# Sample attention of a hybrid decoder step: scores one step behind the key transposes, probabilities scaled by row on the copy out, selection started earlier, first gathers spread

## The reference, cut to what matters

```python
kc = concat([block_means(past_c), block_means(kvc)])        # 128 block means a sample
o_c, imp = compressed_branch(qg, kc, q_pos)                 # softmax over the means; imp = its probabilities, summed
idx, valid = select_blocks(imp, q_pos, n_sel)               # the 8 best of 64 blocks of 64 rows, first and current forced
o_s = sel_attend(qg, kv_sel, idx, valid, q_pos)             # softmax over the selected blocks' rows
o_w, win_new = window_sample(qg, win_buf, kvw, q_pos)       # softmax over the last 512 rows
g = sigmoid(ngate)
o = g[..., 0:1] * o_c + g[..., 1:2] * o_s + g[..., 2:3] * o_w
```

## Time and profile before

| | us |
|---|---|
| median of 3 runs | 1898.01 |
| lowest, highest | 1890.36, 1906.17 |
| the profiled execution | 1902.42 |
| its span in the trace | 1900.3 |
| its busy times: PE, PEld, DVE, ACT, POOL | 1733.5, 1214.2, 955.4, 521.6, 626.8 |
| DMA: bytes moved, mean rate | 248.81 MB, 131 GB/s |

### The profile page before, as it was taken

The page is one execution under the profiler, slowest core; times in us unless marked ns, Lnnn a source line. Parts: engine busy times, 40 slices in busy tenths (PEclk is TensorE's granted clock), DMA queues, the critical chain, the costliest instruction groups (busy, mean ns, idle before and its releaser), DMA issues.

```text
span 1900.3 us, 25684 instructions
## 1 busy us (share of the span) xinstructions
PE 1733.5 (91%) x9632; PEld 1214.2 (64%) x9632; DVE 955.4 (50%) x1708; ACT 521.6 (27%) x1109; POOL 626.8 (33%) x630
## 2 busy tenths in 40 slices
PE   7999999998999689966888889998999999999996
PEld 6777777777877455643555556775467777763332
DVE  5778767773000477744445444233367777750003
ACT  3222212220111345533444445211222223220101
POOL 2344443351000422245555552130055565630000
PEclk9999999998999899987999999999989999999998
DMA  7766666663541100025667668252052322221211
GB/s 243 244 234 228 218 233 220 222 241 109 158 109 34 45 1 1 2 78 165 207 208 222 217 214 257 92 140 75 28 133 67 85 71 74 82 67 56 67 42 50
DMA packets 201014, 248.81 MB, mean 131 GB/s; under 512 B 32201, under 2 KB 173850, under 8 KB 192538
## 3 DMA queue, kind: packets, MB, share of 16 engines
q1 hardware_dynamic: 178556, 137.70, 24.7%
q0 software_dynamic: 21248, 109.46, 16.6%
q10 hardware_dynamic: 1088, 0.00, 0.0%
HBM read 236.09 MB, written 19.29 MB: 134 GB/s over the span
## 4 chain that ended last, share of the span: by engine, by line
PE 74%; DVE 11%; issue 5%; DMA 5%; ACT 4%; another core or an unknown queue 1%; POOL 0%; SPq 0%; DVEq 0%; ACTq 0%; POOLq 0%
PE ps L2200 21%; PE ps L2325 8%; PE ps L2149 5%; DVE mem L1267 5%; DMA mem<-in_cache_cmp_kv,pidx 4%; PE ps L1781 4%; PE ps L2174 4%; PE ps L1770 3%; PE ps L2264 3%; PE ps L1970 3%; PE ps L2113 3%; PE ps L1802 2%; PE ps L2062 2%; PE ps L2029 2%; PE ps L2016 2%
## 5 line engine op out<-in xcount | busy, mean ns | idle before, releaser
L2200 PE MATMUL ps<-mem 128*128 128x288 f32 x1296 | 324.7, 408 | 0.8 <-DVE mem L1205 0.8
L2200 PEld LDWEIGHTS ps<-mem 128*128 128x128 f32 x1296 | 245.5, 191 | 67.7 <-DVE mem L1205 1.0
L759 POOL DMA_INDIRECT mem<-in_cache_sel_kv,sidx x192 | 183.7, 957 | 311.6 <-PE ps L1970 158.8
L1770 PE MATMUL ps<-mem 128*128 128x288 f32 x768 | 208.7, 434 | 16.3 <-DVE mem L1293 15.3
L1770 PEld LDWEIGHTS ps<-mem 128*128 128x128 f32 x768 | 155.7, 205 | 62.2 <-issue 16.2
L1267 DVE TENSOR_TENSOR mem<-mem 128x2048 f32<-128x2048 f32 x56 | 163.7, 2924 | 38.3 <-DMA mem<-in_cache_cmp_kv,pidx 37.6
L722 POOL DMA_INDIRECT mem<-in_cache_cmp_kv,pidx x56 | 90.5, 1616 | 238.3 <-DVE mem L1267 206.6
L2325 PE MATMUL ps<-mem 128*128 128x512 f32 x352 | 163.8, 609 | 0.0
L2174 PE MATMUL ps<-mem 128*64 128x512 f32 x288 | 82.3, 647 | 59.1 <-ACT mem L1048 32.3
L1552 DVE TENSOR_TENSOR mem<-ps,mem 128x512 f32<-128x512 f32 x64 | 44.2, 691 | 159.4 <-PE ps L2174 103.1
L2325 PEld LDWEIGHTS ps<-mem 128*128 128x128 f32 x352 | 63.9, 191 | 80.7 <-issue 80.6
(11 more groups left out here) (372 smaller groups left out, 2776.2 us busy)
## 6 DMA issues: line engine op xcount, KB each, us to landing
mem<-in_cache_sel_kv SPq DMA_DIRECT2D x320, 128.0 KB
mem<-in_w_up SPq DMA_DIRECT2D x44, 512.0 KB, 4.6
mem<-in_w_in SPq DMA_DIRECT2D x32, 512.0 KB, 10.0
mem<-in_w_in SPq DMA_DIRECT2D x14, 1024.0 KB, 9.2
mem<-in_w_down SPq DMA_DIRECT2D x10, 1024.0 KB, 5.0
mem<-in_state_win_kv SPq DMA_DIRECT2D x16, 512.0 KB
out<-in_state_win_kv POOLq DMA_DIRECT2D x8, 1008.0 KB, 15.7
mem<-in_x_prompt SPq DMA_DIRECT2D x8, 512.0 KB, 5.4
```

The lines of the kernel that those rows point to most:

```text
L759: pool.indirect_dma_start(kring[kq % NKR][:, j, :], None, pool_rows, bass.IndirectOffsetOnAxis(sidx[:, i:i + 1], 0)).then_inc(pg_g[kq % NK ...
L1770: mm = t.matmul(ps[:, 2 * (u % 2) + a, 0:NHF], lhs(k), hT[:, k, a * NHF:(a + 1) * NHF], start=(k == 0), stop=(k == KD - 1))
L2200: mm = t.matmul(ps[:, bank, 0:NHF], lhs[:, k, :], rhs[:, k, :], start=(first and k == 0), stop=(k == KD // 2 - 1), skip_group_check=True)
```

## The change

Scores of step n are now issued at the end of step n+1 (`scores`), after the next piece's transposes; keys are copied out by half, each half with its own count, into three buffers in turn (the third in `avm` and `scanm`, free by then). The probabilities are no longer multiplied by gate over sum (`e_scale` is gone): selected and window values are added up side by side in `obank`, now two banks in turn, and `e_out` multiplies by row as it copies out and adds the compressed branch, which is computed by itself (`e_cv`, `e_cmp`). P(m) has one PSUM bank in place of two. `LAG` is 14 in place of 16. The selection's first two parts are one step earlier and two others one step later on PE. The 12 early gathers stand one after each second step of the prompt's attention. POOL waits for the states' stores before it issues the window's copies, since both now share one semaphore.

```diff
-LAG = NC + 6
+LAG = NC + 4
-        kTs = [view(2 * PGC * P).rearrange("p (g n) -> p g n", g=2) for _ in range(2)]
+        kTs = [[view(PGC * P) for _ in range(2)] for _ in range(2)]
+        kTs.append([avm[:, :, :, :].rearrange("p i r c -> p (i r c)"), scanm[:, 0:PGC * P]])
-        obank = ps[:, 6, :]
+        obank = [ps[:, 5 + q, 0:2 * P] for q in range(2)]
...
@@ POOL
+            pool.wait_ge(state_out, 32 * HH)
             for b in range(SB):
                 pool.dma_start(win_s[0, b, 0:WIN - ST].rearrange("w h g d -> w (h g d)"),
...
-            for kq in range(KAHEAD):
-                e_gather(kq)
+            early = [(kq, (j,)) for kq in range(KAHEAD) for j in K_POOL]
             for m, (i, gp, r, br) in enumerate(STEPS):
...
+                if m % 2 and 16 < m < 16 + 2 * len(early) + 1:
+                    e_gather(*early[(m - 16) // 2])
@@ ACT
-                    act.wait_ge(ek_ok, kq + 1)
-                    if kq >= 2:
-                        bb, cc = divmod(kq - 2, NPC + 1)
+                    if kq >= 3:
+                        bb, cc = divmod(kq - 3, NPC + 1)
                         act.wait_ge(es_ok, NC * bb + cc + 1)
-                    a.activation(kTs[kq % 2], ps[:, 0:2, :], ACT.Copy).then_inc(ekT_ok, 1)
+                    for gp in range(2):
+                        act.wait_ge(ek_ok, 2 * kq + gp + 1)
+                        a.activation(kTs[kq % 3][gp], ps[:, gp, :], ACT.Copy).then_inc(ekT_ok, 1)
...
-                    if c == 3:
+                    if c == 2:
                         e_c2(b + 1)
...
-                if c < 4 and 0 < b <= SB:
-                    e_exp(b - 1, [c] if c < 3 else [3, 4])
+                if 1 <= c < 5 and 0 < b <= SB:
+                    e_exp(b - 1, [c - 1] if c < 4 else [3, 4])
@@ DVE
-            def e_scale(b, pieces):
-                for k in pieces:
-                    for q, (a, n) in enumerate(PIECES[k]):
-                        x = sc[b % 2][:, a:a + n]
-                        ins = v.tensor_scalar(x, x, est[:, b % 2, 20 + (q > 0):21 + (q > 0)], None, ALU.mult)
-                    ins.then_inc(epn_ok, 1)
+            def e_cmp(b):
+                dve.wait_ge(cv_ok, b + 1)
+                v.tensor_scalar(ocmp[b % 3], cbank[:, 256:384], gateq[:, b, 0:1], 1.0 / CB, ALU.mult, ALU.mult).then_inc(ocmp_ok, 1)
             def e_out(b):
                 dve.wait_ge(epv_ok, NC * (b + 1))
+                dve.wait_ge(ecf_ok, b + 1)
+                dve.wait_ge(ocmp_ok, b + 1)
+                o, w = ocmp[b % 3], obank[b % 2]
+                link(v.scalar_tensor_tensor(o, w[:, 0:P], est[:, b % 2, 20:21], o, ALU.mult, ALU.add))
                 for g in range(G):
...
+                if c == 1 and b < SB:
+                    e_cmp(b)
                 if b + 1 < SB:
-                    if c == 4:
+                    if c == 3:
                         e_c4(b + 1)
@@ PE
             def e_c1(b):
-                wait(pe, pq_ok, b)
+                wait(pe, ocmp_ok, b)
...
+            def e_cv(b):
+                pe.wait_ge(c10_ok, b + 1)
+                pe.wait_ge(pq_ok, b + 1)
+                for gp in range(2):
+                    mm = t.matmul(cbank[gp * S:(gp + 1) * S, 256:384], pscT[:, gp * S:(gp + 1) * S],
+                                  cmt[:, b, KV + gp * P:KV + (gp + 1) * P], start=True, stop=True)
+                mm.then_inc(cv_ok, 1)
...
+            def scores(n):
+                b, c = divmod(n, NC)
+                kq = b * (NPC + 1) + c
+                wait(pe, esc_ok, n - 1)
+                for gp in range(2):
+                    out = ps[64 * gp:64 * gp + 64, 2 + n % 2, :]
+                    if c <= NPC:
+                        pe.wait_ge(ekT_ok, 2 * kq + gp + 1)
+                        mm = t.matmul(out, qbd[:, b, gp, :], kTs[kq % 3][gp], start=True, stop=True)
...
-                    wait(pe, ekT_ok, kq)
                     for gp in range(2):
+                        wait(pe, ekT_ok, 2 * kq + gp - 1)
+                        bank = gp
...
-                    pe.wait_ge(epn_ok, NP * bb + min(cc // 2, NP - 1) + 1)
-                    wait(pe, epT_ok, m - 1)
+                    pe.wait_ge(eexp_ok, NP * bb + min(cc // 2, NP - 1) + 1)
+                    wait(pe, epT_ok, m)
...
+                if 0 < s <= NC * SB:
+                    scores(s - 1)
+                if b < SB and c == 1:
+                    e_cv(b)
                 if b + 1 < SB:
+                    if c == 2:
+                        e_c1(b + 1)
                     if c == 3:
-                        e_c1(b + 1)
-                    if c == 4:
                         e_c3(b + 1)
-                    if c == 6:
+                    if c == 7:
                         e_c7(b + 1)
-                    if c == 8:
+                    if c == 9:
                         e_c9(b + 1)
```

More of the change, by code:

```diff
@@ L229, in build @@
         at[0] = a_vcz
-        psm, psg, pscT = view(P), view(P), [view(P) for _ in range(2)]
+        psm, pscT = view(P), view(P)
+        ocmp = [view(P), view(P), hmask[:, :]]
         pair, imp, imr, pen32 = view(NSB), view(NSB + 1), view(NSB + 1), view(NSB + 1)
@@ L779, in _ @@
                     if kq >= KAHEAD:
[L780 removed]
+                        wait(pool, ek_ok, 2 * (kq - NKR + 1))
                         e_gather(kq)
@@ L1018, in e_c7 @@
                 act.wait_ge(c7_ok, b + 1)
-                if b >= 2:
-                    act.wait_ge(epv_ok, NC * (b - 2) + 1)
-                a.activation(pscT[b % 2], cbank[:, 384:512], ACT.Copy).then_inc(c10_ok, 1)
+                wait(act, cv_ok, b)
+                a.activation(pscT, cbank[:, 384:512], ACT.Copy).then_inc(c10_ok, 1)
             def e_exp(b, ks):
@@ L1315, in states @@
                 d = dec[h % 2]
-                wait(dve, hgo_out, 32 * h)
+                wait(dve, state_out, 32 * h)
                 for i in range(PT):
@@ L2089, in e_c9 @@
                 t.matmul(cbank[:, 64:64 + NSB + 1], rmatT[:, :], pen32[0:G * ST, :], start=True, stop=True).then_inc(c9_ok, 1)
+            def e_cv(b):
[5 more added lines that the diff above has]
+                mm.then_inc(cv_ok, 1)
             def e_values(m):
                 bb, cc = divmod(m, NC)
+                out = obank[bb % 2]
                 if cc == 0:
-                    wait(pe, eo_ok, bb)
-                    pe.wait_ge(c10_ok, bb + 1)
-                    t.matmul(obank[:, 0:P], identb[:, :], zerob[:, :], start=True, stop=False, skip_group_check=True)
-                    for gp in range(2):
-                        t.matmul(obank[gp * S:(gp + 1) * S, 0:P], pscT[bb % 2][:, gp * S:(gp + 1) * S],
-                                 cmt[:, bb, KV + gp * P:KV + (gp + 1) * P], start=False, stop=False, skip_group_check=True)
+                    wait(pe, eo_ok, bb - 1)
+                    t.matmul(out[:, 0:P], identb[:, :], zerob[:, :], start=True, stop=False, skip_group_check=True)
+                    t.matmul(out[:, P:2 * P], identb[:, :], zerob[:, :], start=False, stop=False, skip_group_check=True)
                 pe.wait_ge(epT_ok, m + 1)
@@ L2106, in e_values @@
                 if cc <= NPC:
-                    parts = [(j, gp, vring[vq % NVR][:, j, gp * P:(gp + 1) * P]) for j in range(PGC) for gp in range(2)]
+                    parts = [(j, gp, int(cc == NPC), vring[vq % NVR][:, j, gp * P:(gp + 1) * P])
+                             for j in range(PGC) for gp in range(2)]
                 else:
-                    parts = [(br, gp, kvt[0:S, PT, (C_VS, C_VW)[br] + gp * P:(C_VS, C_VW)[br] + (gp + 1) * P])
+                    parts = [(br, gp, br, kvt[0:S, PT, (C_VS, C_VW)[br] + gp * P:(C_VS, C_VW)[br] + (gp + 1) * P])
                              for br in range(2) for gp in range(2)]
                 rows_in = P if cc <= NPC else S
-                for j, gp, values in parts:
-                    mm = t.matmul(obank[gp * S:(gp + 1) * S, 0:P], pTs[m % 2][0:rows_in, j, gp * S:(gp + 1) * S], values,
+                for j, gp, br, values in parts:
+                    mm = t.matmul(out[gp * S:(gp + 1) * S, br * P:(br + 1) * P], pTs[m % 2][0:rows_in, j, gp * S:(gp + 1) * S], values,
                                   start=False, stop=(cc == NC - 1 and j == 1), skip_group_check=True)
                 mm.then_inc(epv_ok, 1)
+            def scores(n):
[7 more added lines that the diff above has]
+                        mm = t.matmul(out, qbd[:, b, gp, :], kTs[kq % 3][gp], start=True, stop=True)
+                    else:
+                        for br in range(2):
+                            mm = t.matmul(out[:, br * S:(br + 1) * S], qbd[:, b, gp, :], kT[:, br, gp, T:N], start=True, stop=True)
+                mm.then_inc(es_ok, 1)
             pe.wait_ge(on_ok, PT * NH // 2)
```

83 lines of the change are left out of this document (34 added, 49 removed).

## The result

The changed kernel takes 1881.97 us in the median of 4 runs (1880.90 to 1884.99), the kernel before beside it 1902.09: a ratio of 0.989, with a 95% interval of 0.986 to 0.993. The forecast was 1843 us with a range of 1816 to 1878, so the sign was right and the size was not: about 20 us won in place of 55. The profiled execution took 1882.35 us (span 1880.6) where that of before took 1902.42, so the two traces can be laid side by side.

What follows compares the result with a forecast made beforehand. It took PE with its waits to set the sample stage's time. Gains of 11, 6, 34.5 and 3.2 made 55 us off 1902.4, 1847.7, or 1843 us against the median of 1898.0; range 1816 to 1878.

Steps and rivals of the forecast that it cites:

- Early gathers: Ahead of the sample stage: PE's 11.26 us wait behind 12 gathers goes, gaining 11 us (10 to 12).
- First 14 steps: Start of the sample stage: 56.2 us falls to 50 at 3.2 a step, gaining 6 us (-4 to 13).
- Steps 14 to 79: Middle of the sample stage: 280.5 us falls to 246, a sample from 43.9 to 38 us, gaining 34.5 us.
- Covers the copy and a hand-off that is 1.35 late: Between key copy and scores: some 2.4 us more PE work removes the 1.05 us wait and longer ones.
- 0.4 for what the slack doesn't cover: Steps 14 to 79: 0.4 us of a sample's 38, beside 34 of work and waits of 2.6 and 1.
- The new wait for `e_c1`: In each sample's selection, PE waits for `e_cmp` on DVE: 2.6 us, from 1.9 undisturbed up to 7.6.
- `e_c9` (1): In each sample's selection, PE waits at `e_c9` for `e_c8` on DVE: 0.3 to 1.6 us, taken as 1.
- Values alone: End of the sample stage: 14 steps with values alone in place of 16, 1.61 us each, gaining 3.2 us.
- The second output bank and the scales: Sample stage: 31.5 us of DVE scaling goes, costed at nothing; PE's wait for `e_out` goes, under 1 us a sample.
- (b): Sample stage: late hand-offs and transfers replace the wait, a sample stays at 43 us, 1872 us in all; chance 0.14.
- (d): Selection in each sample: PE, DVE and ACT wait in a ring through `e_c1`, 16 us slower, 1914 us; chance 0.04.
- (c): First 14 steps: PE's clock stays low, costing 4 us instead of gaining 6, 1853 us in all; chance 0.08.

Runs made afterwards that it cites:

- the best version: The changed kernel with plain transfers in place of GpSimd's gathers and the scaling L1509 ahead of the step's penalty and maximum: 1807.01 and 1807.83 us.
- two runs (1890.4 to 1876.6): The kernel before with the early gathers alone, 1890.44 us; the changed kernel with scores back in the step of their own key transposes, 1876.61 us.
- the best order: The changed kernel with the scaling L1509 ahead of the step's penalty and maximum: 1875.55 us with gathers, 1807.01 us with plain transfers.

## Why the prediction was wrong

**Early gathers (11):** right, a little under its bounds (10 to 12). Alone they gave 9.6 us in the trace. That they stand in the attention's steps cost 0.8 us of waits for ACT, within the allowance.

**First 14 steps (6):** 3.8, within its bounds (-4 to 13), but for another reason than T's length. The clock was 0.76 there. Without gathers the same steps take 35.7 us, less than the lower bound of the forecast. Of the 16.8 us between the two, 8.5 are PE's busy time, at a lower clock, 5.0 idle time before T and 3.8 a longer wait for `e_c1`. So the gathers cost this part more than all that the order could win there; how much of it is POOL's pace of 3.7 us a chunk and how much the late posts, no run separates.

**Steps 14 to 79 (34.5):** this is the step that failed, and with it two of its statements. "Covers the copy and a hand-off that is 1.35 late": the slack of 2.4 us was there and the scores' wait went, 36.0 to 1.5 us, but 1.35 was taken from one step as the size of a late hand-off, and half of all posts come out over 1.2 us late, 87 of 296 over 2, up to 5.4 where two bursts follow on each other. Nearly all posts of a burst are late together, and PE itself halts, so that the time came back inside the values and before P, `e_c7` and in part `e_c9`. In the terms of the sum: of a sample's 38 us, 34 of work was right (33.4 in the best version), the new waits had 3.6 and took 2.6, and "0.4 for what the slack doesn't cover" measured about 6.8 (42.86 - 33.42 - 2.62). "So PE with its waits sets the time" was read off busy shares; what made the waits was POOL, though busy for under half of the stretch. The row for it stood in the prediction as a remark ("I take 2.6, since POOL gathers for most of a sample") and was not followed: a clean step of 3.34 us was taken as the rule and the late one behind it as the exception, though the waits in the earlier trace rows spoke of thirty.

Even with the late posts gone, the term would have been wrong as a gain. Without gathers the new order gives 0.3 us a sample, since the wait that it removes came mostly with the gathers, and the one it adds is real. A forecast of 38 us a sample was beaten by both orders then (35.6 and 35.3).

**The new wait for `e_c1` (2.6 a sample):** right in kind and near in size. It is 8.8 us for five samples, 1.8 each, the value of the undisturbed sum (1.9), with and without gathers. Taking it away won 1.7 us a sample. `e_c9` (1): 4.3 for five, 0.9 each.

**Values alone (3.2):** right, 3.3.

**The second output bank and the scales ("at nothing", "under 1 us a sample")**: together with the copy by halves, the moved selection and the two steps fewer (3.3 of it) they are worth some 14 us by the difference of two runs (1890.4 to 1876.6), more than was allowed; which of them was not tried. On POOL the row was right: a gather of the middle part takes 945 ns with the scales gone, where it took 958. P's single bank, which was to hold "just", shows 3.6 us of idle before P in five samples.

**The rivals.** (b) came nearest: it had a sample at 43 us and 1872 us in all, and its words (a late hand-off then meets less slack) are what happened. It named the transfers beside the hand-offs, and these are cleared: DMA carries 270 GB/s without gathers and 221 with them. (d) did not come as a loss. Its sign, over 5 us before L2077, stands in the trace once, in the first part (5.44 at 871.55); in the five samples none is over 1.8 us. (c) came in part, at 0.76, but T ran at 1.09 us in most of these steps and not at 1.97 throughout. Without gathers the same transposes run at 0.94 in these steps, with the lower level (1.2 GHz) for the first 4 us alone, and PE is busy for 30.05 of 35.70 us of them, where it was busy for 38.51 of 52.46. What the prediction cited of the Trainium skill (TensorE: Matmul & The Clock Gate, "Part 4: PE-mode transpose"), that transposes don't count as activity for the clock, finds no support in that row; the scores' matmuls run between them there, so it isn't refuted either.

## What to carry to other kernels

When an engine waits although its source has ended, ask first whether the source's post was late, and look at what else ran in just those moments; a change of order that hides such a wait may only move it. Take away the suspect before you order work around it: here one edit to how pages are fetched was worth 56 to 62 us, where the best order brought 27 with the gathers and 41 without them, and the order's worth could only be read once they were gone. Scores a step behind paid in the first two samples (55.2 us against 62.4 without gathers), where PE had no values to compute between a copy and its scores, and cost 1.5 us in each sample behind them. Where a new order makes an engine wait for a small operation, put that operation ahead of the long ones on its own engine.

## What the runs showed of the hardware

- Indirect gathers on GpSimd right behind one another hold back TensorE's semaphore posts. With three in a row 198 of 296 posts came over 0.3 us late, and with plain transfers of the same bytes from the same queue none of 289. The first late post goes up 0.8 us (median) after the last gather of a burst of three, 0.57 after two, 0.37 after one. TensorE also halts between matmuls that have no waits, longest in a burst of six: up to 0.98 us at a time.
- ScalarE's posts are not held: 20 key copies that ended within a gather released the scores 0.14 or 0.15 us later, as six outside did. VectorE's rises that the trace has are on time too (28 within gathers, 0.02 us at the most).
- The cost is not linear: 0, 0, 1 and 7 us a sample of 35 for none, one, two and three in a row a block; two with a plain transfer between them cost 0.
- A plain transfer of 128 KB takes GpSimd 0.54 us to issue, a gather of as much 0.94 with 0.30 between two. The Trainium skill (DMA: Bandwidth & Descriptors, "SWDGE vs HWDGE vs iDMA") says that both kinds, when GpSimd issues them, have their descriptors written by software on a GpSimd core. The runs show the two to differ, in the time of one and in what they do to TensorE's posts; for a choice between them these numbers decide.
- Which path TensorE's posts and the gathers share was not tried.
